# A transformer block in float32 on one core: the first six weight loads of the second block wait for one semaphore instead of two

## The reference, cut to what matters

```python
def peer(h, p):                       # T = 256 tokens, 8 heads, 16 experts each
    ...
    def block(args):
        xb, ib, gb = args
        act = jax.nn.gelu(jnp.einsum('td,thkd->thk', xb, u_tab[ib]), approximate=False)
        return jnp.einsum('thk,thkd->td', gb * act, v_tab[ib])
...
x_next = x_next + g2 * peer(modulate(x_next, p['norm2_g'], sh2, sc2), p)
...
for l in range(DEPTH_2):              # second block
    h = rms_norm(x, norm_mix_w[l])
    x = x + hybrid_mixer(h, w_in[l], ...)
```

## Time and profile before

| | us |
|---|---|
| median of 3 runs | 2255.3 |
| lowest, highest | 2251.44, 2258.5 |
| the profiled execution, device time | 2256.77 |
| its span, from the first to the last instruction | 2255.0 |

### The profile page before, as it was taken

How to read it: one execution, slowest core, us unless ns; L and a number is a source line. 1 busy time by engine, 2 the same in 40 slices (tenths; PEclk the granted TensorE clock), 3 DMA queues, 4 the chain that set the end, 5 groups by cost and what they waited for, 6 DMA issues and landing times.

```text
span 2255.0 us, 27054 instructions
## 1 busy us (share of the span) xinstructions
PE 2013.2 (89%) x9644; PEld 1480.9 (66%) x9644; DVE 1368.6 (61%) x2736; ACT 1000.8 (44%) x1810; POOL 1051.0 (47%) x844
## 2 busy tenths in 40 slices
PE   7898989877878778787899999999999999998998
PEld 1586667843333333333489877789988987778997
DVE  3677675476666676665427753267762885325776
ACT  2531444422121221312345688455564568845555
POOL 2272357654435444443298666810018865682000
PEclk9899899889899998999899999999999999999999
DMA  9141566399999999999565444545555544454553
GB/s 346 59 131 54 188 231 235 92 397 421 421 422 421 421 421 421 421 421 422 234 193 178 131 150 159 179 151 194 180 170 173 178 140 141 157 180 165 189 179 112
DMA packets 111446, 534.39 MB, mean 237 GB/s; under 512 B 12496, under 2 KB 12880, under 8 KB 77904
## 3 DMA queue, kind: packets, MB, share of 16 engines
q1 hardware_dynamic: 67104, 244.72, 32.6%
q0 software_dynamic: 38720, 275.96, 29.7%
q10 hardware_dynamic: 5488, 11.98, 1.6%
HBM read 531.49 MB, written 1.11 MB: 236 GB/s over the span
## 4 chain that ended last, share of the span: by engine, by line
PE 57%; DMA 23%; DVE 7%; ACT 6%; issue 3%; POOL 2%; another core or an unknown queue 0%; ACTq 0%; DVEq 0%; SPq 0%; POOLq 0%
PE psum L821 56%; DMA pair_rows<-in_peer_uv,arena 10%; DMA arena<-in_peer_uv,arena 7%; DMA wring<-in_peer_uv,arena 5%; ACT w_hi L1303 2%; PE psum L878 2%; POOL w_lo L2601 1%; ACT arena L1314 1%; POOL w_lo L2599 1%; DMA wring<-in_w_ada 1%; ACT arena L1626 1%; DVE arena L2344 1%; ACT arena L1571 0%; DVE arena L2360 0%; DVE small_values L2358 0%
## 5 line engine op out<-in xcount | busy, mean ns | idle before, releaser
L2599 POOL TENSOR_TENSOR w_lo<-wring,w_hi 128x512 fp32r<-128x512 f32 x282 | 384.8, 1365 | 555.1 <-ACT w_hi L1303 506.5
L1303 ACT ACTIVATE w_hi<-wring 128x1024 fp32r<-128x1024 f32 (+1 forms) x414 | 434.3, 1054 | 342.0 <-PE psum L821 305.2
L821 PE MATMUL psum<-w_hi,a_hi 128*128 128x512 f32 (+1 forms) x1056 | 421.0, 399 | 18.6 <-POOL w_lo L2601 9.4
L821 PE MATMUL psum<-arena 128*128 128x512 f32 (+7 forms) x1142 | 352.3, 465 | 74.5 <-ACT arena L1506 47.2
L821 PE MATMUL psum<-w_lo,a_hi 128*128 128x512 f32 (+1 forms) x1056 | 409.8, 388 | 0.0
L821 PE MATMUL psum<-w_hi,a_lo 128*128 128x512 f32 (+1 forms) x1056 | 409.5, 388 | 0.0
L2601 POOL TENSOR_TENSOR w_lo<-wring,w_hi 128x512 fp32r<-128x512 f32 x282 | 395.7, 1403 | 0.0
L821 PE MATMUL psum<-a_hi,w_hi 128*128 128x256 f32 x1312 | 379.4, 289 | 5.8 <-DVE a_lo L1777 3.5
L821 PE MATMUL psum<-a_lo,w_hi 128*128 128x256 f32 x1312 | 374.9, 286 | 0.0
L821 PE MATMUL psum<-a_hi,w_lo 128*128 128x256 f32 x1312 | 374.9, 286 | 0.0
L821 PEld LDWEIGHTS psum<-arena 128*128 128x128 f32 (+2 forms) x1142 | 190.7, 203 | 217.4 <-issue 154.1
(11 more groups left out here) (253 smaller groups left out, 2392.2 us busy)
## 6 DMA issues: line engine op xcount, KB each, us to landing
wring<-in_w_up SPq DMA_DIRECT2D x88, 512.0 KB, 3.4
wring<-in_w_xbc SPq DMA_DIRECT2D x48, 512.0 KB, 3.4
wring<-in_w_dn SPq DMA_DIRECT2D x44, 512.0 KB, 3.3
wring<-in_w_adaT SPq DMA_DIRECT2D x32, 512.0 KB, 4.3
wring<-in_w_qkv SPq DMA_DIRECT2D x32, 512.0 KB, 3.6
wring<-in_w_z SPq DMA_DIRECT2D x32, 512.0 KB, 3.3
wring<-in_w_g SPq DMA_DIRECT2D x32, 512.0 KB, 3.3
wring<-in_w_ps SPq DMA_DIRECT2D x32, 512.0 KB, 3.3
```

The costliest lines, as they stand in the source:

```text
L821: mm = lambda o, a, b, start, stop: nc.tensor.matmul(o, a, b, start=start, stop=stop, skip_group_check=True)
L1303: a.reaches(A(w_hi[:, n % SPLIT_RING, 0:width], wring[:, c % RING, 0:width], ACT.Copy), hi_ready, n + 1)
L2599: nc.gpsimd.tensor_tensor(w_lo[:, r, 0:half], wring[:, c % RING, 0:half], w_hi[:, r, 0:half].bitcast(F32), ALU.subtract)
```

## The change

For the first six chunks of the second block, SP no longer waits for `pair_dot`. It waits for the ring slot's last pick to be used, as before. No instruction moves on any engine and none is added; SP's row of six loads had the waits `weights_lo_ready, pair_dot, pair_used` and now has `weights_lo_ready, pair_used`.

```diff
             if second_block <= c < second_block + RING:
                 sp.wait_ge(S("pair_used"), wring_freed(c % RING))
-                sp.wait_ge(S("pair_dot"), PICKS - 1)
             if c >= RING:
                 if c - RING in split_turn:
                     sp.wait_ge(*low_done(split_turn[c - RING]))
```

## The result

The changed kernel takes 2257.41 us (median of 20 runs, 2251.36 to 2265.71), the kernel before 2252.52 us (median of 20, 2248.29 to 2258.5). The ratio is 1.0024, with a 95% interval from 1.0016 to 1.0031: about 5 us slower, within the 0.3% that I had called about what can be told from no change, yet clear of zero with 20 runs each. The profiled execution has a span of 2259.8 us.

A forecast was written before the change was run, and what follows sets the result against it. The end of PEER was taken as set by the landing of pick 252's gather and PE's eight picks behind it. Gain 0, PE +4.1 at start and +4.4 at end; +5 on the median 2255.3 gave 2260.3, range 2255.0 to 2264.5.

The forecast's parts named there:

- Nothing is gained: Early w2_qkv loads bring 0 us: ACT's rounding and POOL's first `w_lo` are released by other events, not by these loads.
- SP's release: SP's first w2_qkv load goes out at 1085.3 in place of 1102.23, once `pair_used` alone holds it, 17 us earlier.
- full-clock case: With picks 240 and 241 at full clock, release comes 3 us earlier, 34 weight packets precede pick 252, PE 5.5 us late.
- One-to-one turns: On a shared DMA engine, gather and weight queues alternate about one packet for one, whatever the size; 25 weight packets precede pick 252.
- The lagging engine: One DMA engine, some 10 us behind fifteen finished ones, sets the last gathers' landing and gets 48 packets from six chunks.
- First data 1.5 us after the issue: The first early weight data move about 1.5 us after SP's issue, at 1086.8 (1083.8 if PE runs at full clock).
- PE: PE starts pick 248 at 1100.9 in place of 1096.80 (+4.1 us) and ends +4.4 us; half clock again costs one pick 3.4.
- ACT: ACT shifts by 7.8 us against 4.4, with slack of 2.93: 0.5 us too late for the first half of x.
- The full price: Rival: all 48 weight packets pass ahead of pick 252, PE starts 7.8 us late; +7.8 to +9.3 us; chance 0.20.
- hidden: Rival: gathers already in the rings pass first and weights fill the fifteen idle engines; 0 us, 2255.3; chance 0.14.
- unequal turns: Rival: five gather packets pass for three of weights, 15 weight packets precede pick 252; 2.5 us, 2257.8; chance 0.07.
- faster: Rival: later starts avoid PE's half clock of 1098 to 1100 and gathers lose little; gain 1 or 2 us; chance 0.03.

The follow-up runs named there:

- thin: Changed kernel, but the six early loads bring only the first 128 of 1024 columns of each chunk; 1.0007 [0.9996, 1.0018] of the kernel before.
- mid: Kernel before, but the six loads wait for the dot product of pick 252 in place of pick 254; 1.0001 [0.9991, 1.0012] of before.
- again: The changed kernel, unaltered, measured once more; 1.0020 [1.0011, 1.0029] of the kernel before.
- double: Changed kernel, with SP also copying each of the six early chunks to a scratch tensor in DRAM; 1.0046 [1.0031, 1.0060] of the kernel before.
- two_early: Kernel before, but slots 0 and 1 are loaded early while slots 2 to 5 still wait for pair_dot; 1.0024 [1.0015, 1.0033] of before.
- two_again: The kernel of two_early, unaltered, run a second time; 1.0020 [1.0008, 1.0032] of the kernel before.
- small_early: Changed kernel, but the last eight picks go in batches of 2, 2, 1, 1, 1, 1, not 4, 2, 1, 1; 1.0035 of before.
- later: Kernel before, but the six loads wait until PE has used pick 251; 1.0002 [0.9993, 1.0011] of before.
- small_wait: Kernel before, pair_dot wait kept, but the last eight picks go in batches of 2, 2, 1, 1, 1, 1, not 4, 2, 1, 1; 0.9983 of before.
- small_again: The kernel of small_wait, unaltered, run once more; 0.9992 [0.9982, 1.0003] of the kernel before.

## Why the prediction was right, point by point

- **Nothing is gained.** Right, and shown to within 1 or 2 us: the load as early but thin gains nothing, and loads 1.8 us later than before lose nothing.
- **SP's release.** Expected at 1085.3 or, with PE at full clock, 3 us earlier. It came 17.20 us after pick 240, the full-clock case (1082.4 on the clock of before).
- **One-to-one turns.** Right: 73 beside 68 packets, dots 3.76 us apart, and single rows in turn on the engine that works alone (1107.4 to 1108.33 us of after).
- **The lagging engine.** Right: in before 30 gather packets pass one after the other from 1093 to 1102 us, at 6.1% of 16 engines, and the last dot waits for the last of this queue (1102.9).
- **Price of a packet.** 0.16 us; 16 packets made 2.56 us, and 8 per gather 1.26. All 48 made 7.6 us at pick 255, where the prediction has 7.8 (48 x 0.16 is 7.7).
- **First data 1.5 us after the issue.** This is the term that was mis-sized, and no row of the prediction has it. In the trace of before, with idle engines, the first packets start 1.0 us after the issue and the bulk from 1.7 us on, and the estimate of 1.5 lies between them; in after, with busy ones, the first starts 3.5 us after it (rows above). The dots say the same of the lagging engine: pick 249 is late by only 0.65 us, four packets, though its data are busy until some 4.7 us after the issue. So 28 packets got in ahead of pick 252 (4.5 / 0.16) and not the 34 of the full-clock case. The same error made me expect 1.3 and 2.6 us in mid, where 0 and 1.3 were seen.
- **PE.** With the full-clock release I expected a start 5.5 us late and an end 5.5 late; measured 4.5 and 5.2 (5.0 in again). The sum for the profiled execution of before, at half clock, gave 4.1 and 4.4. The traces of after don't have the late release that this sum was made for, and they have fewer packets ahead of pick 252 than the other. The +5 for the median was set between the two sums, so that it is so close to the measured 4.9 is in part luck; each step of its mechanism was seen. After the longer idle PE's half clock cost 2.4 us (10.99 against 8.6) where I counted 1.7, and PE did not idle again before pick 252.
- **ACT.** Expected 0.5 us too late for the first squares. Its slack shrank to 0.51 us and was not used up: its shift was 7.6 us and PE's 5.2, where I had set 7.8 and 4.4.
- **The absolute time.** 2260.3 was forecast on a median before of 2255.3 from three runs; 20 runs put that at 2252.52. The difference was right, the base was 3 us high.
- **The rivals.** The full price falls by the pace of 3.76 us and by double, hidden by the dots of every kernel with early loads, unequal turns by the single turns of the engine that works alone (their five to three was an assumption of mine that no run shows; the runs show one to one), faster by the time and by thin.

Not explained are the times of two_early, two_again, double and small_early, which lie some 2 to 4.5 us above what the traces of their ends show.

## What to carry to other kernels

A wait that looks idle can be what keeps one stream out of the way of another. Before a load is moved earlier, look at who reads it first and what releases that reader. Here it was not the load, and the move only took DMA time from what was in flight. The cost was counted by the rows that passed ahead of the transfer that somebody waited for (28 packets, 4.5 us, ahead of pick 252), not by all the rows that were moved (48), and the early load was free once it stood behind the last transfer on the path (mid, released by the dot of pick 252: 1.0001).

## What the runs showed of the hardware

- Two queues on one DMA engine took turns packet by packet, one 4 KB row for one 8 KB row, at 0.16 and 0.31 us (after); with 512 B rows (thin) a turn added some 0.03 us (1.2 us over some 40 turns). In a copy from DRAM to DRAM (double) the packet was 32 KB and 1.21 us, for one turn all the same.
- The engines didn't run level: at the end of the gathers of before fifteen were through by 1093 and one went on to 1103 at some 25 GB/s (one packet of 0.31 us after the other), and it set when the last gathers landed. The same was seen from 1093 to 1094 in later, small_wait and small_again (25 to 33 GB/s), and the last dot came at 38.15 to 38.18 in these three and in before. Each trace has a longer step ahead of pick 254 (3.44 us in before, 35.69 less 32.25): in before two packets of the instruction queue (q14) pass between 1097 and 1103, for 0.9% of 16 engines over 6 us, 0.86 us, which would explain it if they ran on that one engine.
- A load issued while the gathers kept the engines busy (after) showed its first packet 3.5 us later, where with idle engines (before) it took 1.0 us.
- PE's granted clock was 0.50 for a part of its work behind an idle time in most traces, and 1.00 throughout in others, of the same kernel too: the same 32 matmuls of picks 248 to 255 took 13.8, 15.5 and 16.5 us in three traces of one kernel. So single traces differed by 2.6 us at this place alone. A matmul (128x512, f32) took 0.43 us at 1.00 and 0.82 us at 0.50 (before: the 12 from 1107.14 on, and the 8 from 1076.96 to 1083.53).
